# One encoder block on one core: the convolution's input projection moved ahead of the latents, and who copies the latents out of PSUM

## The reference

```
u = RMSNorm(h)
proj = u @ w_in          # 4928 columns: query latent 512 | kv latent 256 | rotary key 64 | conv a 1024 | conv b 1024 | gates 2048
q, kv from RMSNorm(latents) @ w_uq, w_ukv ; k_r = rotary(key) ; attn = softmax attention (8 heads) @ w_o_attn
c = a * sigmoid(b)                                   # gated linear unit
c = depthwise conv of width 31 over time (c) + bias  # one filter per channel
conv = silu(LayerNorm(c)) @ w_conv_out
h = h + (sigmoid(gate_a) * attn + sigmoid(gate_c) * conv) @ w_out
h = h + relu(RMSNorm(h) @ w_mlp_in)^2 @ w_mlp_out ; output RMSNorm(h) without the meta tokens
```

## Time and profile before

| | us |
|---|---|
| median of 3 runs | 1373.28 |
| the three runs | 1371.81, 1373.28, 1397.13 |
| span of the profiled execution | 1370.2 |
| PE busy / DVE busy in that span | 1291.8 / 706.3 |

### The profile page before, as it was taken

How to read it: one execution, slowest core, us unless ns; L and a number is a source line. 1 busy time by engine, 2 the same in 40 slices (tenths; PEclk the granted TensorE clock), 3 DMA queues, 4 the chain that set the end, 5 groups by cost and what they waited for, 6 DMA issues and landing times.

```text
span 1370.2 us, 18509 instructions
## 1 busy us (share of the span) xinstructions
PE 1291.8 (94%) x7181; PEld 1118.4 (82%) x7181; DVE 706.3 (52%) x743; ACT 461.5 (34%) x681; POOL 458.5 (33%) x244
## 2 busy tenths in 40 slices
PE   5999989999936999999999999999999999999996
PEld 4888878888836888987888888888888888888885
DVE  4117999999998877777453123111111132243224
ACT  5233111222214666663442134222222233322235
POOL 1443324444332334334522322222233222332224
PEclk8999999999977999999999999999999999999999
DMA  5222212233210101103335121222222121112212
GB/s 175 71 74 65 62 46 61 82 109 107 88 35 12 28 20 36 42 16 108 108 105 203 62 62 49 69 67 61 61 61 61 62 77 62 61 62 65 74 46 92
DMA packets 123907, 96.17 MB, mean 70 GB/s; under 512 B 9695, under 2 KB 106013, under 8 KB 123852
## 3 DMA queue, kind: packets, MB, share of 16 engines
q1 hardware_dynamic: 121548, 89.12, 21.9%
q10 hardware_dynamic: 2304, 6.29, 1.2%
HBM read 85.96 MB, written 9.44 MB: 70 GB/s over the span
## 4 chain that ended last, share of the span: by engine, by line
PE 69%; DVE 14%; issue 12%; ACT 3%; DMA 1%; SPq 0%; POOL 0%; DVEq 0%; ACTq 0%
PE psum L316 38%; PE psum L1673 23%; DVE acc L943 8%; PE psum L1550 2%; PE psum L1580 2%; PE psum L1438 1%; PE psum L1515 1%; DMA xt<-in_x_prompt 1%; PE psum L1562 1%; ACT junk L822 1%; DVE ptlo L1041 1%; ACT prob L605 1%; DVE olo L1106 0%; PE psum L1403 0%; DVE negmax L1029 0%
## 5 line engine op out<-in xcount | busy, mean ns | idle before, releaser
L303 POOL TENSOR_TENSOR wlo<-raw,whi 128x1024 fp32r<-128x1024 f32 (+2 forms) x144 | 361.9, 2513 | 743.4 <-ACT whi L298 743.2
L943 DVE SCALAR_TENSOR_TENSOR acc<-cs,convw,acc 128x799 f32<-128x799 f32 x232 | 291.2, 1324 | 0.0
L298 ACT ACTIVATE whi<-raw 128x1024 fp32r<-128x1024 f32 (+2 forms) x144 | 146.7, 1019 | 306.6 <-PE psum L1673 207.0
L1232 DVE TENSOR_TENSOR hidlo<-hid,hidhi 128x1536 fp32r<-128x1536 f32 x32 | 82.1, 2566 | 169.8 <-ACT hidhi L800 169.8
L316 PE MATMUL psum<-uhi,whi 128*128 128x512 f32 x592 | 154.5, 342 | 10.7 <-DVE cs L974 8.8
L316 PE MATMUL psum<-ulo,whi 128*128 128x512 f32 x592 | 154.1, 342 | 0.0
L316 PE MATMUL psum<-uhi,wlo 128*128 128x512 f32 x592 | 153.9, 341 | 0.0
L1673 PE MATMUL psum<-whi,hidhi 128*128 128x512 f32 x384 | 149.4, 389 | 0.0
L1673 PE MATMUL psum<-whi,hidlo 128*128 128x512 f32 x384 | 149.4, 389 | 0.0
L1673 PE MATMUL psum<-wlo,hidhi 128*128 128x512 f32 x384 | 149.4, 389 | 0.0
L1242 DVE SCALAR_TENSOR_TENSOR hid<-psum,rbc 128x768 f32 (+1 forms) x32 | 30.6, 958 | 216.6 <-PE psum L316 216.6
(11 more groups left out here) (221 smaller groups left out, 2044.1 us busy)
## 6 DMA issues: line engine op xcount, KB each, us to landing
raw<-in_w_in SPq DMA_DIRECT2D x38, 512.0 KB, 4.1
raw<-in_w_mlp_in SPq DMA_DIRECT2D x32, 512.0 KB, 4.0
raw<-in_w_mlp_out SPq DMA_DIRECT2D x32, 512.0 KB, 3.6
gates<-gout ACTq DMA_DIRECT2D x16, 384.0 KB, 2.3
gin<-gates SPq DMA_DIRECT2D x16, 384.0 KB, 3.1
raw<-in_w_o_attn SPq DMA_DIRECT2D x8, 512.0 KB, 4.1
raw<-in_w_conv_out SPq DMA_DIRECT2D x8, 512.0 KB, 3.9
raw<-in_w_out SPq DMA_DIRECT2D x8, 512.0 KB, 3.7
```

Source lines behind the costliest of these rows:

```text
L298: nc.scalar.activation(whi[:, c % 2, 0:w], raw[:, c % 4, 0:w], ACT.Copy).then_inc(hi_ready, 1)
L303: gp.tensor_tensor(out=wlo[:, c % 2, 0:w], in0=raw[:, c % 4, 0:w], in1=whi[:, c % 2, 0:w].bitcast(F32), op=ALU.subtract).then_inc(lo_ready, 1)
L943: ins = nc.vector.scalar_tensor_tensor(out=a, in0=src, scalar=w, in1=a, op0=ALU.mult, op1=ALU.add)
L1232: nc.vector.tensor_tensor(out=hidlo[c % 2][:, :, :], in0=hid[:, ds(i * 8 + 2 * c, 2), :], in1=hidhi[c % 2][:, :, :].bitcast(F32), op=ALU.s ...
```

## The change

The 16 convolution units come first, then the 8 latent and key units, then the 16 gate units. SP, ACT, POOL and PE are all written in this order.

- PSUM: the convolution units use pairs 0, 1, 2, 3 in turn (b in 0 and 2, a in 1 and 3). PE waits for the gated unit of two tiles ago and no longer for the one before.
- ACT squares each latent unit straight from PSUM and copies it out itself (new L543, L544), and DVE's copy is gone. PE waits for both before it reuses the pair. The first square waits for all eight gated units, since `sqt` and `sg` share memory.
- ACT's later steps on the latents (root of the kv sum, split of the key, six roundings) stand behind certain gate units (`LATENTS`), where before they stood between the first convolution units. `gout` moves to the memory of `sg`.
- DVE: the gated units and the taps are written out without loops, in the order of the tuple (2, 2, 1, 2, 2, 1, 2, 7): so many parts after each gated unit. Then come the rotary key, both reciprocals and the six scalings, one part, the key's and the latents' subtractions as ACT delivers them, and all that is left of tiles 5 and 6. Taps 28 to 30 of tile 6 and its combine now stand ahead of attention.
- POOL waits for the six latent subtractions before it clears two tiles of attention, whose memory holds the latents.
- The first two units on PE have 272 columns in their second half where before they had 256.

Cut to its core:

```diff
-U_QKV = 0
-U_CONV = 8
-U_GATE = U_CONV + 2 * KD
+U_CONV = 0
+U_QKV = U_CONV + 2 * KD
+U_GATE = U_QKV + 8
...
-        gout = at("gout", [P, 2, TQ], F32, V0 + 62464)
+        gout = at("gout", [P, 2, TQ], F32, V0 + 75008)
...
-            for n in range(1, 6):
-                columns(win, 4 * (n // 4), 0, n % 4, slice(n * P, (n + 1) * P))
+            def conv_units(i):
+                for c in range(4):
+                    if isinstance(i, int) and i == 0 and c == 0:
+                        continue
+                    first = C_B if c % 2 == 0 else C_A
+                    columns(win, U_CONV, i, c, ds(i * (2 * P) + (first + (c // 2) * P), P))
+            rolled(sp, 4, conv_units, peel=1)
+
+            for n in range(6):
+                columns(win, U_QKV + 4 * (n // 4), 0, n % 4, slice(n * P, (n + 1) * P))
             sp.dma_start(rcos[:, :], t["rope_cos"]).then_inc(tables_landed, 16)
             sp.dma_start(rsin[:, :], t["rope_sin"]).then_inc(tables_landed, 16)
             for e in range(2):
-                sp.wait_ge(lo_ready, 6 + e - 3)
+                sp.wait_ge(lo_ready, U_QKV + 6 + e - 3)
...
+            def conv_step(i):
+                for c in range(4):
+                    if not (isinstance(i, int) and i == 0 and c == 0):
+                        hi_unit(act, U_CONV, i, c + 1)
+                    if c % 2 == 0:
+                        act.wait_ge(unit_used, i * 4 + (U_CONV + c + 1))
+                        wait(act, glu_ready, i * 2 + (c // 2 - 1))
+                        nc.scalar.activation(sg[:, c // 2], psum[:, c, 0:TK], ACT.Sigmoid).then_inc(sg_ready, 1)
+            rolled(act, 4, conv_step, peel=1)
+
+
             for n in range(8):
                 if n in (5, 6):
                     act.wait_ge(dup_landed[n - 5], 16)
-                if n > 0:
-                    hi_unit(act, 0, 0, n + 1) if n < 3 else hi_unit(act, 4, 0, n + 1 - 4)
+                hi_unit(act, U_QKV, 0, n + 1)
                 if n < 6:
-                    act.wait_ge(raw_q, n + 1)
+                    act.wait_ge(unit_used, U_QKV + n + 1)
+                    if n == 0:
+                        act.wait_ge(glu_ready, KD)
                     wait(act, sq_sum, n - 1)
-                    src, w = (qraw[:, n], TQ) if n < 4 else (kvraw[:, n - 4], TK)
-                    nc.scalar.activation(sqt[:, n % 2, 0:w], src, ACT.Square).then_inc(q_sq, 1)
-                if n == 7:
-                    act.wait_ge(unit_used, 8)
-                    for b in range(4):
-                        o = b ^ 1
-                        ins = nc.scalar.activation(krsw[32 * o:32 * o + 32, :], psum[32 * b:32 * b + 32, 2, 0:TK], ACT.Copy)
-                    ins.then_inc(kr_sw, 1)
+                    dst, w = (qraw[:, n], TQ) if n < 4 else (kvraw[:, n - 4], TK)
+                    nc.scalar.activation(sqt[:, n % 2, 0:w], psum[:, n % 2, 0:w], ACT.Square).then_inc(q_sq, 1)
+                    nc.scalar.activation(dst, psum[:, n % 2, 0:w], ACT.Copy).then_inc(raw_q, 1)
+            act.wait_ge(unit_used, U_GATE)
+            for b in range(4):
+                o = b ^ 1
+                ins = nc.scalar.activation(krsw[32 * o:32 * o + 32, :], psum[32 * b:32 * b + 32, 2, 0:TK], ACT.Copy)
+            ins.then_inc(kr_sw, 1)
...
+            LATENTS = {(0, 1): (kv_root,), (1, 2): (kr_split,), (1, 3): (lambda: latent_hi(0), lambda: latent_hi(1)),
+                       (2, 0): (lambda: latent_hi(2), lambda: latent_hi(3)),
+                       (2, 1): (lambda: latent_hi(4), lambda: latent_hi(5))}
...
-                        act.wait_ge(qkv_lo, 6)
+                        act.wait_ge(sq_sum, 6)
                     nc.scalar.activation(gout[:, c % 2], psum[:, c % 2, 0:TQ], ACT.Sigmoid,
                                          bias=vcol("b_gate", i * 4 + c)).then_inc(gate_ready, 1)
                     act.wait_ge(gate_ready, i * 4 + (c + 1))
                     dst = gates[ds(i * 4 + c, 1)].rearrange("a p n -> p (a n)") if not isinstance(i, int) else gates[i * 4 + c]
                     act.dma_start(dst, gout[:, c % 2]).then_inc(gate_stored[c % 2], 16)
-            rolled(act, 4, gate_step, peel=1, last=1)
+                    if isinstance(i, int):
+                        for step in LATENTS.get((i, c), ()):
+                            step()
+            rolled(act, 4, gate_step, peel=4)
...
-            for n in range(6):
-                dve.wait_ge(unit_used, n + 1)
-                dst, w = (qraw[:, n], TQ) if n < 4 else (kvraw[:, n - 4], TK)
-                nc.vector.tensor_copy(dst, psum[:, n % 2, 0:w]).then_inc(raw_q, 1)
...
+            def glu(j):
+
+                dve.wait_ge(sg_ready, j + 1)
+                dve.wait_ge(unit_used, U_CONV + 2 * j + 2)
+                s = sg[:, j % 2]
                 for o, c0, n in ((CS_PROMPT, 0, T_PROMPT), (CS_META2, META0, T_META + T_SAMPLE), (0, META0, T_META)):
-                    ins = nc.vector.tensor_tensor(out=dst(o, n), in0=psum[:, 1, c0:c0 + n], in1=s[:, c0:c0 + n], op=ALU.mult)
+                    ins = nc.vector.tensor_tensor(out=cs[:, j, o:o + n], in0=psum[:, 2 * (j % 2) + 1, c0:c0 + n],
+                                                  in1=s[:, c0:c0 + n], op=ALU.mult)
                 ins.then_inc(glu_ready, 1)
 
             dve.wait_ge(pads_zero, 2)
-            kr_los(), recip_q()
-            glu(0, 1)
-            for j in range(KQ):
+            LAST = KD - 1
+            parts = [(tile, c) for tile in range(LAST) for c in range(4)]
+
+            def conv_parts(n):
+                for tile, c in parts[:n]:
+                    if c == 0:
+                        dve.wait_ge(glu_ready, tile + 1)
+                    conv_part(tile, c)
+                del parts[:n]
+            for j, n in enumerate((2, 2, 1, 2, 2, 1, 2, 7)):
+                glu(j)
+                conv_parts(n)
+            rotate_key()
+            recip_q(), recip_kv()
+            for j in range(KQ + KKV):
                 latent_scale(j)
-            latent_lo(0)
-            glu(0, 3)
-            latent_lo(1), latent_lo(2), latent_lo(3)
-            recip_kv(), latent_scale(4), latent_scale(5)
-            dve.wait_ge(glu_ready, 1)
-            conv_part(0, 0)
-
-            def conv_step(i, order):
-
-                dve.wait_ge(glu_ready, i * 2)
-                for what in order:
-                    if isinstance(what, str):
-                        glu(i, 1 if what == "first glu" else 3)
-                    else:
-                        conv_part(i - 1, what)
-            conv_step(1, ("first glu", 1, 2, "second glu", 3))
-            latent_lo(4)
-            latent_lo(5)
-            with dve.Fori(2, 4) as i:
-                conv_step(i, (0, "first glu", 1, 2, "second glu", 3))
-
-            dve.wait_ge(glu_ready, KD)
-            with dve.Fori(3, 6) as tile:
-                for c in range(4):
-                    conv_part(tile, c)
-            for c in range(3):
-                conv_part(6, c)
-            for k in range(24, 28):
-                tap(6, k, 6 * TAPS + k)
-
-
-            LAST = KD - 1
+            conv_parts(1)
+            kr_los()
+            for j in range(4):
+                latent_lo(j)
+            conv_parts(1)
+            latent_lo(4), latent_lo(5)
+            conv_parts(len(parts))
...
-                for k in range(29, TAPS):
-                    tap(6, k, 6 * TAPS + k)
-                combine(6, LAST * TAPS)
-                dve.wait_ge(conv_done, LAST)
...
-            start_pair(0, lambda step: tap(6, 28, 6 * TAPS + 28) if step == 1 else None)
+            start_pair(0)
...
-                c0, w = ((0, T_PROMPT), (SAMP0, T_SAMPLE))[seg]
+                c0, w = ((0, T_PROMPT), (META0, T_META + T_SAMPLE))[seg]
...
-            for n in range(2, 6):
-                pe.wait_ge(raw_q, n - 1)
-                unit(4 * (n // 4), 0, n % 4, n % 2, u, QSEG if n < 4 else KSEG)
-            for e in range(2):
-                unit(4, 0, 2 + e, 2, u, KSEG, k_tiles=range(4 * e, 4 * e + 4), first=e == 0, last=e == 1)
-                if e == 0:
-                    sum_squares(pe, 0, TQ, 4)
-            pe.wait_ge(raw_q, 6)
-
             def conv_step(i):
                 for c in range(4):
-                    if c % 2 == 0:
-                        wait(pe, sg_ready, i * 2 + c // 2)
-                    else:
-                        wait(pe, glu_ready, i * 2 + c // 2)
-                    unit(U_CONV, i, c, c % 2, u, KSEG)
+                    if isinstance(i, int) and i == 0 and c < 2:
+                        continue
+                    wait(pe, sg_ready if c % 2 == 0 else glu_ready, i * 2 + (c // 2 - 1))
+                    unit(U_CONV, i, c, c, u, KSEG)
+            rolled(pe, 4, conv_step, peel=1)
...
+
+            for n in range(6):
+                if n < 2:
+                    pe.wait_ge(sg_ready if n == 0 else glu_ready, KD - 1)
+                else:
+                    pe.wait_ge(raw_q, n - 1)
```

(43 more changed lines are left out.)

52 lines of the change are left out of this document (8 added, 44 removed).

## The result

| | median us | runs | span of the profiled execution |
|---|---|---|---|
| before | 1372.97 | 1371.81 to 1397.13 (4) | 1370.2 |
| after | 1393.81 | 1392.81 to 1394.63 (4) | 1392.8 |

The ratio is 1.0153, with a 95% interval of 1.0137 to 1.0169. The kernel became 21 us slower; the forecast was 26 us faster.

The account below looks back on a forecast made before the run. PE sets the pace, but waits for DVE's late taps before attention. Moving the queries' product from 420.25 to 394.8 gains 25.4 us, attention 1.0: 26.4 off the median 1373.3 gives 1346.9 us; eight-in-ten range 1336 to 1361.

Parts of the forecast that it names:

- What bounds the kernel: PE sets the pace nearly everywhere; its largest wait, 23.8 us for `qt`, comes from DVE being late for attention with its taps.
- PE's timetable: PE's new order without waits: convolution units to 167.6, latent and key units to 228.1, all sixteen gates to 362.9 us.
- four pairs: Convolution units over four PSUM pairs: PE's 8.8 us of waits for gated units go, but are not booked as gain.
- ACT's copies: Six latent copies of about 1 us moved from DVE to ACT: neither gain nor loss; PE stalls 1 us.
- DVE's load: DVE starts at 47.4 with 247.3 us of content and 90 of collisions, done at 385 without any wait.
- the price of a collision: Delay of DVE by each two-input POOL operation: 1.8 us on average, 50 of them; possible range zero to 2.44.
- The new wait for ACT's roundings: At the latents' subtractions, after the ninth gate, DVE idles some 9 us until 309.9, with 62 taps queued behind.
- Attention: Taps 29, 30 and the combine leave the chain at attention's start, 443.50 to 448.4: gain 1.0 us.
- for the stall above and one held-up `wlo`: At the ninth gate: 1.5 us of PE lateness added to 304.5, giving 306.0 for roundings 3 and 4.
- the rival that came true: A `wlo` held behind 31 or 24 unbroken taps after the eighth gated unit; two such holds give 1395; chance 0.05.
- the second and third rivals: Held `wlo` make PE late at the ninth gate: some 12 us, about 1359 (0.17); or grown to a loss (0.05).

Follow-up runs that it names:

- a_break8: The changed kernel with every eighth tap of tiles 0 to 6 waiting for the tap just before it, which breaks DVE's string: 1346.1 us, ratio 0.9803 to the kernel before.
- b_halves: The kernel before; meant to issue taps of tiles 3 and 4 as two, but the condition was never true, so unchanged: 1396.7, 1397.2, 1373.3 and 1396.1 us.
- with halves: The kernel before with each tap of tiles 3 to 5 issued as two instructions of 400 and 399 elements: 1424.54 us, ratio 1.0377.
- a_fill: The changed kernel with breaks at every eighth tap and one convolution part of eight taps put between the query latents' subtractions: 1340.89 us, ratio 0.9767.
- a_best: The changed kernel with eighth-tap breaks, eight taps between query latents' subtractions, and tile 6's taps 28 to 30 and combine moved behind the queries' product: 1338.81 us, ratio 0.9755.
- a_hi_first: The changed kernel with ACT's order altered: for even `c` both weight splits stand ahead of the sigmoid, for odd `c` none: 1358.37 us, ratio 0.9895.

## Why the prediction was wrong

- *What bounds the kernel* was read rightly: DVE's taps, late for attention. In a_break8, where nothing is held for long, PE waits 21.3 us for `qt` (17 to 24 were forecast), no unit waits for a gated unit, and the product ends at 394.07 (394.8).
- *PE's timetable, four pairs, ACT's copies, DVE's load and the price of a collision* therefore came out: 26.2 us of gain at the join against 25.4. The new wait for ACT's roundings is 6.5 + 1.0 = 7.5 us (9), there as in the kernel after with 12.0. These are not each measured alone; their sum is. (Two sums on the way are slightly off: the terms behind 309.9 add up to 83.7 and not 83.9, and DVE at the key's subtraction comes to 290.8 and not 292. Neither matters for the result.)
- *Attention*, forecast as 1.0 us of gain, is a loss of 0.9: from the product to the end a_break8 takes 1344.9 - 394.07 = 950.8 us, before 1370.2 - 420.25 = 949.95.
- *The step that failed* is the 1.5 us "for the stall above and one held-up `wlo`", and with it the chance of 0.05 for the rival that came true. It took holds for accidents: 3 of 29 before, "in the straight-line stretches of taps before, as in the last 26, none was held". They follow a rule. Before, the `wlo` that got in met strings of at most 5.45 us (bar one at 192.97, whose string ended just then); the exceptions in the earlier trace rows had ages of 8.8 and 5.8. And the last 26 taps (393.23 to 419.4) prove nothing, since no POOL operation came to them after the one at 392.83. POOL's next row in the kernel before:

```profile
426.40 1.84 POOL L303 TENSOR_TENSOR wlo<-raw,whi 128x768 fp32r<-128x768 f32 x1 [31.96 <-ACT whi L298]
```

The change moved seven arrivals to 6.2 and above and put strings of 29 and 22 taps against the latent stage. In place of the 1.5 us, the holds cost 47.7 us (1393.81 - 1346.1). PE's waits for `wlo` before 300 us, named as the sign of the second and third rivals from 10 us on:

```profile
PE psum L316 <- POOL wlo L303: 38.5, 5, 16.8
```

That the holds are the cause, and not only beside it, is shown by the breaks: same work, same order, 45 to 48 us.
- The rival's own working (24 us for each long hold, two of them: 1395) has the right mechanism, and its 1395 is within 1.2 us of the 1393.81. That closeness is in part luck: there were seven holds of 5 to 23 us and not two of 28, the two of the latent stage are worth 31.6 us and the other five 16.1, and only the total, 47.7, meets its 48. Its chance could have been put higher by working out at what ages `wlo` would arrive in DVE's strings and setting them beside the ages in the timeline of before.

By the Trainium skill, page "SBUF — State Buffer", section "SBUF: two separate sides", the loser of the shared port is blocked until the other engine's instruction ends. For DVE waiting on POOL the trace agrees (a tap grows by 2.1 for a `wlo` of 2.44); for POOL waiting on DVE it doesn't: of the 23.27 us at 416.11, 21.6 pass before the combine, 22 taps.

## What to carry to other kernels

Where VectorE runs a long string of instructions and GpSimd's results are waited for, look up in both timelines at what age of the string GpSimd's operations arrive; an operation that takes ten times its usual time and ends just where the string ends is the sign. Let VectorE wait on its own last instruction every few instructions: here every eighth took 48 us off. It isn't free: in the kernel before, where little was held, every fourth cost 9 us. And before a change that shifts arrivals is judged, count the margin by which the present ones get in: 0.4 us here (5.45 let in, 5.8 held), and copies of 0.8 us on another engine used it up.

## What the runs showed of the hardware that was not expected

- GpSimd is shut out by a string of back-to-back taps of VectorE (two-input instructions, behind at most two one-input ones) once that is some 5.5 to 5.9 us old, until it ends: up to 24.8 us with whole taps (314.94 in b_halves) and 27.9 with halves. With whole taps it was let in within 3.3 us at ages up to 5.64 (108.98 in a_break8) and held at 5.8 and above, unless the string happened to end just then; with halves it was held at 5.5 (272.76). The exceptions are the two `wlo` before subtractions in a_fill and their like in a_best.
- What ended a string was a wait of VectorE, even one of 0.04 us (the break before 57.30 in a_break8), or the gated unit's product, which reads one of its two inputs from PSUM: the hold at 57.65 in the kernel after is over when L965 runs at 65.16.
- A one-input operation of GpSimd is held as well: `TENSOR_SCALAR` took 21.34 us, and 0.85 at 183.30 in a_hi_first.
- Two profiles of the same program can differ by a hold: in the kernel before, a `wlo` near 306 us met the first opening tap in one and the second in the other, the next one was held for 24.8 us or let in (2.66), and the spans are 1394.9 and 1370.2.
